# A two-layer diffusion backbone: tables of the Fourier front split later and its groups prepared ahead, attention steps of four tiles for the first and the last query block

## What is computed

```python
def _fourier_mixer(h, w_out, b_out):                # layer 0, latent and context
    hf = h.reshape(b, s, 4, 256)
    mixed = jnp.fft.fft2(hf, axes=(1, 3), norm='ortho').real
    return mixed.reshape(b, s, 1024) @ w_out + b_out
...
def one_block(args):                                # layer 1, for each of 8 blocks of 128 queries
    qpos = j * 128 + jnp.arange(128)
    kpos = (j - 1) * 128 + jnp.arange(384)
    valid = (abs(qpos[:, None] - kpos[None, :]) <= 128) & (kpos >= 0) & (kpos < seq_len)
    s_win = jnp.where(valid, q @ k_window, -inf)     # 16 heads, 3 key tiles of 128
    s_ctx = q @ k_ctx                                # 2 key tiles of 128
    p = softmax([s_win, s_ctx, sink])[..., :-1]
    return p_win @ v_window + p_ctx @ v_ctx
```

## Time and profile before

| | |
|---|---|
| time, median of 3 runs | 2476.28 us (2474.57 to 2476.38) |
| the profiled execution | 2472.16 us, span 2470.2 us |
| PE busy | 2302.4 us, 93% of the span |
| DVE, ACT, POOL busy | 1745.0 us (71%), 1111.8 us (45%), 1014.7 us (41%) |
| PE weight loads | 1911.1 us (77%) |
| mean granted clock of TensorE | 0.977 of 2.4 GHz |
| moved by DMA | 192.71 MB, mean 78 GB/s |

### The profile page before, as it was taken

How to read it: one execution, slowest core, us unless ns; L and a number is a source line. 1 busy time by engine, 2 the same in 40 slices (tenths; PEclk the granted TensorE clock), 3 DMA queues, 4 the chain that set the end, 5 groups by cost and what they waited for, 6 DMA issues and landing times. The chain is left out here.

```text
span 2470.2 us, 37317 instructions
## 1 busy us (share of the span) xinstructions
PE 2302.4 (93%) x11638; PEld 1911.1 (77%) x11638; DVE 1745.0 (71%) x2866; ACT 1111.8 (45%) x2002; POOL 1014.7 (41%) x795
## 2 busy tenths in 40 slices
PE   4988989999999999999679898898989999999998
PEld 2667867888888888888577677776768888888887
DVE  4553587777777777777765688882577777777776
ACT  4453443333333333333453488883334343434343
POOL 0002623344333344333256566675534544444443
PEclk9999999999999999999789899999999999999999
DMA  6434202223222222222312211104111212021112
GB/s 240 170 138 166 90 26 69 68 76 102 68 81 80 68 76 89 81 76 77 114 35 103 90 40 34 33 28 171 51 43 34 68 34 68 34 68 34 68 34 94
DMA packets 79135, 192.71 MB, mean 78 GB/s; under 512 B 6864, under 2 KB 15440, under 8 KB 75728
## 3 DMA queue, kind: packets, MB, share of 16 engines
q1 hardware_dynamic: 76128, 184.92, 21.8%
q10 hardware_dynamic: 2928, 6.82, 0.7%
HBM read 174.94 MB, written 16.78 MB: 78 GB/s over the span
## 5 line engine op out<-in xcount | busy, mean ns | idle before, releaser
L790 POOL TENSOR_TENSOR ht<-ht,l_side 128x512 f32<-128x512 f32 x224 | 300.6, 1342 | 929.6 <-ACT l_side L873 921.3
L51 PE MATMUL l_z_ps<-nh,l_w1h 128*128 128x512 f32 (+1 forms) x1280 | 477.3, 373 | 15.3 <-POOL l_w1l L58 5.4
L1147 DVE SCALAR_TENSOR_TENSOR ht<-l_yy_ps,mod,ht 128x512 f32<-128x512 f32 x672 | 465.9, 743 | 26.7 <-PE l_yy_ps L1438 25.8
L52 PE MATMUL l_z_ps<-nl,l_w1h 128*128 128x512 f32 (+1 forms) x1280 | 474.8, 371 | 0.0
L53 PE MATMUL l_z_ps<-nh,l_w1l 128*128 128x512 f32 (+1 forms) x1280 | 474.6, 371 | 0.0
L1436 PE MATMUL l_yy_ps<-l_ah,l_w2h 128*128 128x512 f32 x896 | 354.3, 395 | 8.0 <-DVE l_al L58 4.0
L1437 PE MATMUL l_yy_ps<-l_al,l_w2h 128*128 128x512 f32 x896 | 350.3, 391 | 0.0
L1438 PE MATMUL l_yy_ps<-l_ah,l_w2l 128*128 128x512 f32 x896 | 350.0, 391 | 0.0
L873 ACT ACTIVATE l_side<-l_yy_ps,mod 128x512 f32<-128x512 f32 x224 | 153.9, 687 | 343.6 <-PE l_yy_ps L1438 343.6
L51 PEld LDWEIGHTS l_z_ps<-nh,l_w1h 128*128 128x128 f32 x1280 | 243.3, 190 | 62.4 <-issue 8.5
L53 PEld LDWEIGHTS l_z_ps<-nh,l_w1l 128*128 128x128 f32 x1280 | 243.5, 190 | 40.5
(11 more groups left out here) (240 smaller groups left out, 4554.0 us busy)
## 6 DMA issues: line engine op xcount, KB each, us to landing
l_aw<-ada SPq DMA_DIRECT2D x128, 256.0 KB, 3.0
l_w1f<-w SPq DMA_DIRECT2D x64, 512.0 KB, 3.3
l_w2f<-w SPq DMA_DIRECT2D x64, 512.0 KB, 4.9
maw<-ada SPq DMA_DIRECT2D x24, 1024.0 KB, 5.2
queries<-qhl SPq DMA_DIRECT2D x16, 512.0 KB, 2.8
stage<-queries SPq DMA_DIRECT2D x32, 256.0 KB, 2.6
early<-fnet_w SPq DMA_DIRECT2D x11, 512.0 KB, 4.4
early<-wo SPq DMA_DIRECT2D x11, 512.0 KB, 3.6
```

The costliest lines, as they stand in the source:

```text
L51: pe.matmul(out, lh, rh, start=first, stop=False)
L52: pe.matmul(out, lh, rl, start=False, stop=False)
L790: pool.tensor_tensor(h, h, side[(i - 1) % 2][:], ALU.add).then_inc(s_add, 1)
L1147: dve.scalar_tensor_tensor(out=h, in0=y_ps[m][:], scalar=mod[:, layer, G2, c, 0:1], in1=h, op0=ALU.mult, op1=ALU.add).then_inc(s_acc, 1)
```

## The change

In the front, `tabf` is no longer split in `prologue`. The rounded parts are now ScalarE copies in `fnet_mix`, the remainders VectorE subtractions behind the first group's preparation, and TensorE waits for each table where it first uses it. A one-element square root ahead of the squares loads ScalarE's table of that function earlier. `prep(g+2, 0)` is done inside `y_out(g, 0)`, two groups ahead, instead of between the halves of `sets`; two banks of the next group are taken out (`evict`) ahead of `y_out(g, 1)`; `ada_columns` moves off the end of `token_sums`, and `feature_sums` starts when six of eight remainders are there. In attention, steps whose block is the first or the last (`edge`) work on four tiles, with scores, mask, exponential and division over 512 keys instead of 640, and their turned tiles alternate between the two banks. The first pair of blocks is written out, so that the loop has two rounds.

```diff
             def _(act):
                 act.activation(sig[:], vec[:, V_C:V_C + 2 * KC], ACT.Exp, scale=-1.0).then_inc(s_e, 1)
+                act.wait_ge(s_eps, 3)
+                act.activation(warm[:], eps[:], ACT.Sqrt).then_inc(s_warm, 1)
                 for t in range(NT):
...
             def _(dve):
-                for i in range(4):
-                    dve.wait_ge(s_tab[i], 16)
-                    dve.tensor_scalar_mul(tabh[:, i], tabf[:, i], 1.0).then_inc(s_th, 1)
-                    dve.wait_ge(s_th, i + 1)
-                    lo_part(dve, tabl[:, i], tabf[:, i], tabh[:, i]).then_inc(s_tl, 1)
...
+                def table(i):
+                    act.wait_ge(s_tab[i], 16)
+                    act.activation(tabh[:, i], tabf[:, i], ACT.Copy).then_inc(s_th, 1)
...
                 def sets(g, i):
+                    ahead = 2 if g and i == 0 else 0
+                    for j in range(4):
+                        if g == 0 and i == 0 and j == 2:
+                            prep(1, 0)
+                        if j >= ahead:
+                            evict(g, i, j)
+                        high(g, i, j)
...
                 def y_out(g, m):
...
+                    if m == 0 and g + 2 < GR:
+                        prep(g + 2, 0)
...
                     sets(g, 0)
-                    if g + 1 < GR:
-                        prep(g + 1, 0)
                     ada_rows(3 * g + 1)
                     sets(g, 1)
...
                     ada_rows(p)
+                    if g + 1 < GR:
+                        for j in range(2):
+                            evict(g + 1, 0, j)
                     y_out(g, 1)
...
                 def feature_sums(g, p):
-                    pe.wait_ge(s_uvl, g * 8 + 8)
+                    pe.wait_ge(s_uvl, g * 8 + 6)
...
+        def tiles(jj, n):
+            return (0, 1, 2, 4) if edge(jj, n) else range(KB)
...
+        def heads_at(jj, n, kb):
+            if not edge(jj, n):
+                return [kb] if kb < 4 else []
+            return [3] if kb == 4 else [kb]
...
             step(0, 0, True, True, start=True)
-            with eng.Fori(0, PAIRS - 1) as jj:
+            for n in range(1, NQ + 1):
+                step(0, n, True, True)
+            with eng.Fori(1, PAIRS - 1) as jj:
```

More of the change, by code:

```diff
@@ L306, in y_out @@
                     act.activation(chunk[:, LAT:T], y_ps(m, 2)[:, 0:256], ACT.Copy, scale=2.0 ** -8).then_inc(s_yh, 1)
+                for i in range(3):
+                    table(i)
                 prep(0, 0)
+                table(3)
                 ada_rows(0)
@@ L396, in _ @@
                 prep(0, 0)
+                for i in range(1, 4):
+                    table(i)
+                dve.wait_ge(s_id, 16)
+                dve.reduce_sum(sel[:], ident[:].rearrange("p (j c) -> p c j", c=32)[:, 0:2, :], axis=AX.X).then_inc(s_sel, 1)
                 prep(0, 1)
@@ L2084, in step @@
                 def step(jj, n, with_a, with_q, start=False):
-                    for kb in range(KB):
-                        slot = (n + kb) % 2
+                    for kb in tiles(jj, n):
+                        _, slot = place(jj, n, kb)
                         act.wait_ge(s_pt, at(jj, n, KB, kb + 1))
-                        act.wait_ge(s_o, at(jj, n, KB, kb - 1))
-                        act.activation(pth[slot][:], bank(kb)[:], ACT.Copy).then_inc(s_ph, 1)
-                        if kb and with_a:
-                            head(jj, n + 2, kb - 1)
+                        act.wait_ge(s_o, taken(jj, n, kb))
+                        act.activation(pth[slot][:], bank(jj, n, kb)[:], ACT.Copy).then_inc(s_ph, count(jj, n, kb))
+                        for h in ([2, 3] if edge(jj, n) and kb == 4 else [kb - 1]) if kb and with_a else []:
+                            head(jj, n + 2, h)
                         if kb == 0 and not start:
@@ L2136, in step @@
                 def step(jj, n, with_a, with_q, start=False):
-                    for kb in range(KB):
-                        slot = (n + kb) % 2
+                    for kb in tiles(jj, n):
+                        _, slot = place(jj, n, kb)
                         dve.wait_ge(s_ph, at(jj, n, KB, kb + 1))
-                        lo_part(dve, ptl[slot][:], bank(kb)[:], pth[slot][:]).then_inc(s_pl, 1)
+                        lo_part(dve, ptl[slot][:], bank(jj, n, kb)[:], pth[slot][:]).then_inc(s_pl, count(jj, n, kb))
                         if kb == 0 and (with_a or n + 1 < NQ):
                             recip(jj, n + 1)
-                        if kb == O_AT and not start:
+                        if kb == O_AT and not start and not edge(jj, n):
                             part_o(jj, n - 1)
-                        if kb < 4 and with_a:
-                            head(jj, n + 2, kb)
+                        for h in heads_at(jj, n, kb) if with_a else []:
+                            head(jj, n + 2, h)
+                        if kb == O_AT and not start and edge(jj, n):
+                            part_o(jj, n - 1)
                         if kb == 2 and with_q:
                             part_q(jj, n + 3)
-                    if n % 4 == 2 and not (isinstance(jj, int) and n > 4):
+                    if n % 4 == 2 and not (isinstance(jj, int) and jj and n > 4):
                         window(jj, n // 4 + 1)
@@ L2209, in step @@
                         for h in range(4):
-                            last = pe.transpose(bank(kb)[:, h * P:(h + 1) * P], sc[:, n % SETS, h, kb * P:(kb + 1) * P], ident[:])
-                        last.then_inc(s_pt, 1)
-                        if kb < 4 and with_a:
-                            head(jj, n + 2, kb)
+                            last = pe.transpose(bank(jj, n, kb)[:, h * P:(h + 1) * P], sc[:, n % SETS, h, tile * P:(tile + 1) * P], ident[:])
+                        last.then_inc(s_pt, count(jj, n, kb))
+                        for h in heads_at(jj, n, kb) if with_a else []:
+                            head(jj, n + 2, h)
                         if kb:
-                            values(jj, n, kb - 1)
+                            values(jj, n, 2 if edge(jj, n) and kb == 4 else kb - 1)
                         elif not start:
```

159 lines of the change are left out of this document (111 added, 48 removed).

## The result

| | before | after |
|---|---|---|
| median of 4 runs each | 2476.33 us (2474.57 to 2478.35) | 2440.64 us (2440.07 to 2440.81) |
| the profiled execution | 2472.16 us | 2440.57 us, span 2438.8 us |
| PE busy | 2302.4 us (93%) | 2287.3 us (94%) |

The ratio is 0.9856, with an interval of 0.9841 to 0.9871: the kernel is 35.7 us faster.

What follows compares the result with a forecast made beforehand. TensorE, busy 93%, bounds the kernel, so gains come from its waits in the front and attention, where no engine is full. Front -18.8 and attention -9.4 total -28.2: 2472.2 becomes 2444.0, the median 2476.3 becomes 2448; range 2441 to 2459.

Steps and rivals of the forecast that it cites:

- (1): Start of the front: earlier square root and preparation bring TensorE's first product from 34.17 to 27.6 us; -6.6.
- (2): First token_sums in the front: the map's columns move ahead of the last set and cover most of a 1.85 wait; -1.6.
- (3): Front, group 0: 40.38 us becomes 38.2 despite a new wait of 1.8 for the third bank; -2.2.
- (4): Front, groups 1 and 2: two TensorE waits go, 40.93 becomes 36.4 each; -9.0 for both, +1.6 for low clock left.
- (5): Front, group 3: feature_sums starts with six of eight remainders, so about 1 us of its wait goes; -1.0.
- one seam, steps written out: Attention loop: two rounds have one seam instead of two, -1.5; eight written-out steps cost 8.70 instead of 8.75, -0.4.
- fifth tile dropped: Attention, eight steps lose a tile: five steps -0.5, step 5 of the last pair -0.6, last step 0.95.
- narrow heads, division, start: Attention on 512 keys: six steps with narrow heads -3.0, eight heads ahead of step 0 -1.5, last division shorter by 1.0.
- A: Rival, front: handshakes hold y_ps back and the low clock stays; front -13, total -22, 2454; chance 0.20.
- B: Rival, attention: narrow steps give nothing, or alternating banks add waits; attention -4.5, total -23, 2453; chance 0.14.
- C: Rival, attention: a step shrinks with its tiles; total -37, 2439; chance 0.06.
- D: Rival, attention, slower: TensorE falls to 1.2 GHz in the eight short steps; +48, 2496; chance 0.02.

Runs made afterwards that it cites:

- e15: Changed kernel with only the second group's preparation put back behind the first group's first half; 2443.96 us, +3.2.
- e11: Changed kernel with the two banks taken out ahead of y_out(g, 1) put back behind it, preparation still two groups ahead; 2444.39 us, +3.6.
- e6: Changed kernel with the products for the map's columns back at the end of each token_sums; 2441.13 us against 2440.80 for the unedited copy.
- e7: Changed kernel with the next group's preparation back between the halves of sets and no bank taken out ahead; 2458.87 us, +18.1.
- e4: Kernel before with only the first pair of blocks written out, leaving two loop rounds, five tiles everywhere; ratio 0.9990, 2.5 us faster by the median.
- e10: Changed kernel with scores, mask, exponential and division of the edge steps back on 640 columns, their four tiles kept; 2444.98 us, +4.2.
- e13: Kernel before with the third round written out behind a loop of two, instead of the first pair ahead; stage 1.7 us shorter, median no better.
- e2: Changed front with the attention of the kernel before; 2455.82 us, ratio 0.9923 against the kernel before.

## Why the prediction was right where it was, and where it failed

**The base.** "All is summed against the profiled execution's own time, 2472.16 us, which is 4.1 below the median", and the difference was then added back. This step failed, and it cost 4.1 of the 7.4 us; of the rest the front made 3.2 and attention 0.4, and the rest of the kernel took some 0.2 back. The execution was low because of its front, which the change replaces: 202.53 against 205.8 to 206.4 in six others. So the gain had to be counted from a typical front too; from 206 to 180.5 it is some 25.5 us, and with 9.8 for attention that is 35.3, against 35.7 between the medians. In which executions the front is short, no run shows.

**(1) First product**, -6.6: -6.1 in the trace, right. **(2)**, -1.6: the wait fell from 1.85 to 0.35. The stretch fell by only 0.7 between the two profiled executions (12.82 instead of 13.55), but it took 13.8 to 14.9 in the six later profiles of the old front and 12.3 to 13.7 in those of the changed one, so the term was about right. **(3)**, -2.2 with a new wait of 1.8: -3.2 with 1.74, and -4.7 against the 41.9 of the later profiles. The wait was right in place and size, and no low clock came behind it; the 0.5 for `y_ps` and part of the 35.9 were too much, as in (4). e15 shows that the alternative would be worse.

**(4) Groups 1 and 2** is the term that was mis-sized: -7.4 forecast, -11.5 measured. Three pieces of it, each for both groups. The products of a group were priced at 35.9 us and take 35.1: 0.8 each. The low clock went altogether while I had left 0.8 in. And the wait of 0.5 for a bank of `y_ps` does not exist. The 2.1 per group make the 4.1. The 1.6 for the low clock itself was right: one product, an `ada` unit and three products take 3.66 us in it and 2.12 behind it.

```profile
101.84 0.60 PE L53 MATMUL seq_ps<-tabh,gl 128*128 128x512 f32 x1
...
105.50 0.40 PE L51 MATMUL seq_ps<-tabh,gh 128*128 128x512 f32 x1
...
105.96 0.39 PE L53 MATMUL seq_ps<-tabh,gl 128*128 128x512 f32 x1
...
108.08 0.39 PE L51 MATMUL seq_ps<-tabh,gh 128*128 128x512 f32 x1
```

Of the 0.8 in the 35.9, 0.6 arise because only the waits' own lengths were taken off. A wait of 1.61 costs 1.84 (e11), and the late `gl` cost 2.1 where its row says 1.73: from the last product ahead of it to the next one it is 3.24 us (97.33 to 100.57), with the columns between them. In the changed kernel a product and the same columns take 1.11. The mechanism was half right. That taking out ahead removes the first bank's wait is shown by e11, at 1.8 per group. But "`mrows` no longer stands behind `gh`" names only the first of two things that were late in one place; e6 and e7 show that the columns' new place is worth nothing by itself, and that the preparation of the whole group had been late. **(5)**, -1.0: -0.5, since a wait of 1.29 for `uvl` stayed.

**Attention**, -9.4 forecast and -9.8 measured, is right in the sum only, and that is luck:

```
                                   forecast   measured (stage)
one seam, steps written out          -1.9      -3.1   (before 301.9, e4 298.8)
fifth tile dropped                   -2.05     -3.4   (e4 298.8, e10 295.4)
narrow heads, division, start        -5.5      -3.2   (e10 295.4, after 292.1)
```

"Two rounds instead of three have one seam instead of two" failed: both go, and e13 shows that it is the place of the written-out pair that does it. The dropped tile gives 0.2 per step in the first pair and not 0.1, so it is not wholly outside the cycle, and nothing in place 30 (e10's 8.71). In place 31 it gives 0.7 (e10's 7.98 against 8.69), where I had 0.6, and in the last two steps 1.4 (19.57 in e4, 18.21 in e10) where I had 0.95. "On the cycle lie three masks and one exponential: 0.5" was too much by a third to a half; the prices per operation were right and the steps still gave 0.25 to 0.5, so part of the masks seems to lie beside other work; which, no run shows. The narrower division gave 0.8 where the clock stayed up and nothing where it fell, against my 1.0.

**The rivals.** A (handshakes) fell: the only product into `y_ps` that waits noticeably is the one of group 3, for `uvl`. B fell with e10. C fell: 0.2 per tile in the first pair, 0.7 at the most, and not 1.75. D fell for every short step that makes heads: they ran at a clock of 1.00. In the last two steps it happened on a small scale, in five of nine profiles, and cost 0.8.

## What to carry to other kernels

Before a gain is summed against a profiled execution, ask whether the stage that is to be changed was typical in it; a second profile of the same kernel would have moved this forecast by 4 us. Behind a wait that is to be removed, look for the next thing that is late at the same place: with only the first of them gone, as in e7, the group was longer than before. In a loop of long written steps, compare the step behind each round with its neighbours; its cost is a property of where the code lies, and an unrelated edit can change it by several us.

## What the hardware showed that I had not expected

- A loop's seam of 1.7 us became 3.2 with other code ahead of it, and 5.3 with 24 fulfilled waits more in each of four lists. It shows as idle time that ends with issue; of the 5.3, 1.3 are in the following step, which began at half clock. Behind a written-out copy of the body it was 0.1.
- Waits of 1.61 us left the granted clock at 1.00 (e11), one of 2.36 went with 0.96 over its group (e15), and 1.61 with 2.91 with 0.88 (e7), where TensorE was busy for 4.7 us longer on top of 4.5 us of idle. The length of a wait does not settle it: in e2 the step behind the seam of 3.0 us began at 0.68, and the one behind the seam of 3.3 at 1.00.
- Executions of one program differ by 5 to 7 us (2471.4 to 2478.1 for the kernel before, 2438.0 to 2443.2 for the changed one), and the profiles place the part that I could follow in the front's stretches at 1.2 GHz: the same first group took 40.4 or 41.9 us, at a mean clock of 0.96 or 0.92.
